# Seven quarter products in the first block's gate and up, with its background rows shared between the engines

## The reference, cut to what matters

```
hp = rms_norm(xp, norm_ffn[l]) * (1.0 + sc2_c) + sh2_c
hs = rms_norm(xs, norm_ffn[l]) * (1.0 + sc2_s) + sh2_s
xp = xp + g2_c * swiglu(hp, w_gate[l], w_up[l], w_down[l])
xs = xs + g2_s * swiglu(hs, w_gate[l], w_up[l], w_down[l])
swiglu = (silu(h @ w_gate) * (h @ w_up)) @ w_down
```

## Time and profile before

| | |
|---|---|
| median of three runs | 1569.83 us |
| profiled execution, first to last instruction | 1566.4 us |
| TensorE busy | 1538.6 us, 98% |
| VectorE busy | 1113.9 us, 71% |
| ScalarE busy | 743.6 us, 47% |
| GpSimd busy | 287.6 us, 18% |
| mean granted clock of TensorE | 0.995 |

### The profile page before, as it was taken

The page is one execution under the profiler, slowest core; times in us unless marked ns, Lnnn a source line. Parts: engine busy times, 40 slices in busy tenths (PEclk is TensorE's granted clock), DMA queues, the critical chain, the costliest instruction groups (busy, mean ns, idle before and its releaser), DMA issues.

```text
span 1566.4 us, 26496 instructions
## 1 busy us (share of the span) xinstructions
PE 1538.6 (98%) x10775; PEld 1483.5 (95%) x10775; DVE 1113.9 (71%) x1882; ACT 743.6 (47%) x1236; POOL 287.6 (18%) x344
## 2 busy tenths in 40 slices
PE   8989999999999999999999999999999999999998
PEld 6989788899999999999999899989999999999998
DVE  5657877866779746665467999988688468568453
ACT  3435555653544423442235766676365335335332
POOL 0010111000156524453253023221000000000000
PEclk9999999999999999999999999999999999999999
DMA  9332332132354544444333388875203222222322
GB/s 329 110 109 62 110 103 82 36 122 81 96 168 148 162 128 127 155 136 135 113 116 95 78 180 174 175 151 132 81 28 101 88 81 75 88 81 75 91 68 78
DMA packets 142464, 178.12 MB, mean 114 GB/s; under 512 B 13025, under 2 KB 121257, under 8 KB 141320
## 3 DMA queue, kind: packets, MB, share of 16 engines
q1 hardware_dynamic: 120128, 109.68, 22.3%
q0 software_dynamic: 21888, 66.66, 17.2%
q10 hardware_dynamic: 328, 0.10, 0.0%
HBM read 148.93 MB, written 2.79 MB: 97 GB/s over the span
## 4 chain that ended last, share of the span: by engine, by line
PE 87%; DVE 8%; ACT 2%; issue 1%; DMA 1%; POOL 0%; DVEq 0%; ACTq 0%
PE PS L777 23%; PE PS L779 22%; PE PS L782 22%; PE PS L858 5%; PE PS L860 5%; PE PS L859 5%; PE PS L1185 1%; PE PS L1196 1%; PE PS L1138 1%; DVE PTL L2698 1%; DMA MODA<-in_w_mod 1%; DVE WL L2099 0%; PE PS L1161 0%; DVE TMP L2288 0%; DVE X L2441 0%
## 5 line engine op out<-in xcount | busy, mean ns | idle before, releaser
L777 PE MATMUL PS<-HH,WH 128*128 128x320 f32 (+1 forms) x1168 | 269.6, 312 | 2.8 <-DVE HL L2299 2.2
L779 PE MATMUL PS<-HL,WH 128*128 128x320 f32 (+1 forms) x1168 | 266.1, 309 | 0.0
L782 PE MATMUL PS<-HH,WL 128*128 128x320 f32 (+1 forms) x1168 | 265.4, 308 | 0.0
L2425 DVE SCALAR_TENSOR_TENSOR X<-PS,MODV,X 128x128 f32<-128x128 f32 (+2 forms) x216 | 81.6, 434 | 185.4 <-PE PS L782 185.3
L777 PEld LDWEIGHTS PS<-HH,WH 128*128 128x128 f32 x1168 | 194.5, 188 | 7.5 <-issue 3.5
L779 PEld LDWEIGHTS PS<-HL,WH 128*128 128x128 f32 x1168 | 196.0, 188 | 0.0
L782 PEld LDWEIGHTS PS<-HH,WL 128*128 128x128 f32 x1168 | 195.8, 188 | 0.0
L2099 DVE TENSOR_TENSOR WL<-RAW,WH 128x2048 fp32r<-128x2048 f32 (+2 forms) x56 | 126.6, 2261 | 65.1 <-ACT WH L1503 64.9
L777 PE MATMUL PS<-HIDH,WH 128*128 128x320 f32 x704 | 163.0, 312 | 0.3 <-DVE HIDL L2356 0.3
L1867 ACT ACTIVATE BGW<-BGW,SC 128x512 f32<-128x512 f32 x112 | 80.8, 723 | 173.4 <-DVE BGACC L2247 124.0
L699 POOL TENSOR_TENSOR BGACC<-BGACC,BGW 128x512 f32<-128x512 f32 x97 | 132.4, 1365 | 159.8 <-ACT BGW L1867 158.6
(11 more groups left out here) (409 smaller groups left out, 3206.0 us busy)
## 6 DMA issues: line engine op xcount, KB each, us to landing
BGW<-in_w_mod POOLq DMA_DIRECT2D x112, 256.0 KB, 3.0
RAW<-in_ffn_w_gate SPq DMA_DIRECT2D x22, 1024.0 KB, 5.3
RAW<-in_ffn_w_up SPq DMA_DIRECT2D x22, 1024.0 KB, 5.4
MODA<-in_w_mod POOLq DMA_DIRECT2D x48, 256.0 KB, 3.7
RAW<-in_ffn_w_down SPq DMA_DIRECT2D x16, 768.0 KB, 4.7
RAW<-in_ffn_w_down SPq DMA_DIRECT2D x8, 1024.0 KB, 5.1
RAW<-in_conv_w_pw SPq DMA_DIRECT2D x16, 512.0 KB, 5.3
WL<-RAW POOLq DMA_DIRECT2D x8, 1024.0 KB, 9.8
```

Source lines behind the costliest of these rows:

```text
L777: mm(o, wh, xh, start=first, stop=False)
L779: mm(o, wh, xl, start=False, stop=False)
L782: ins = mm(o, wl, xh, start=False, stop=last)
L2425: ins = V.scalar_tensor_tensor(out=X[:, m, t:t + b - a], in0=tile2(n)[:, bank, a:b], scalar=g, in1=X[:, m, t:t + b - a], op0=ALU.mult, op1 ...
```

## The change

Layer 0's block gets the form of layer 1's: seven quarter products from `up 2` on, 19 units in all, the block ring, chunks of 6, 6, 6 and 4, and eight hidden places. `RING_GAP` skips three places of the ring before the last chunk, so that the ring ends where the next stage's units begin.

The 14 background halves are no longer made by VectorE, ScalarE and GpSimd together.

- 8 halves go through TensorE, 6 in layer 0 and 2 in layer 1. Inside a gate unit, after product 0 and after product 5, four column groups multiply four loaded pieces (`half_rows`). VectorE transposes the result (`turn_half`), and four small matmuls after product 3 of the up unit add it up (`turn_half_rows`). GpSimd loads the pieces to four buffers (`half_loads`); the next four are loaded when the last four have been used.
- 6 halves go as three parts of 1024 columns, one beside each of layer 0's first three chunks of down. VectorE makes the context's sum (`part_first`), ScalarE scales (`part_scaled`), and GpSimd issues a transfer that adds the scaled piece to a sum in SBUF (`part_rows`). It waits for that transfer before it loads a further piece. The three buffers `BGW` share memory with `P5`, `TMP` and `ACTV`, so ScalarE waits for adding transfers before it copies into these (`added`).
- The last half's sum before `pw2`, with two clock-holding matmuls, becomes ten clock-holding matmuls.

```diff
-DOWN_K = ((8, 8, 6), (6, 6, 6, 4))
+DOWN_K = ((6, 6, 6, 4), (6, 6, 6, 4))
-FAST_FROM = (1, 2)
+FAST_FROM = 2
+RING_GAP = 3
+PE_HALVES = {(0, 4): 0, (0, 6): 1, (0, 10): 8, (0, 12): 9, (0, 16): 10, (0, 18): 11, (1, 4): 12, (1, 6): 13}
+PART_AFTER = (8, 14, 20)
+PE_BEFORE = (2, 4, 6)
...
+            if b == last_chunk:
+                place += RING_GAP
...
# GpSimd
+            def half_loads(first, last):
+                for i in range(KT * first, KT * last):
+                    r, k = divmod(i, KT)
+                    if i >= MOD_SLOTS:
+                        pool.wait_ge(sem("modb_used"), (i - MOD_SLOTS) // GROUPS + 1)
+                    l, c0 = divmod(FIRST_BG * D + PE_ORDER[r] * 512, 6 * D)
+                    pool.dma_start(MODB[i % MOD_SLOTS][:], w_mod[l, k * P:(k + 1) * P, c0:c0 + 512]).then_inc(sem("modb_landed"), 16)
+            def part_load(q, k):
+                l, c0 = divmod((PART0 + q) * D, 6 * D)
+                pool.dma_start(BGW[k % 3][:], w_mod[l, k * P:(k + 1) * P, c0:c0 + D]).then_inc(mod_landed[k % 3], 16)
+            def part_rows(q):
+                pool.wait_ge(sem("hid_ready"), PART_AFTER[q])
+                for k in range(3):
+                    part_load(q, k)
+                for k in range(KT):
+                    pool.wait_ge(sem("bgw_scaled"), KT * q + k + 1)
+                    if k:
+                        pool.dma_start(BGACC[1][:], BGW[k % 3][:], accum_op=ALU.add).then_inc(sem("bgw_added"), 16)
+                        pool.wait_ge(sem("bgw_added"), 16 * ((KT - 1) * q + k))
+                    if k + 3 < KT:
+                        part_load(q, k + 3)
# TensorE, in fast_pair
+                def between(i):
+                    if turn is not None and i == 3:
+                        turn_half_rows(tile2(n2), turn)
+                    if part is not None and i == 3:
+                        part_sums(tile2(n2), part)
+                    if rows is not None and i in (0, 5):
+                        half_rows(tile2(n2), rows, i // 5)
+            def half_rows(ps, j, step):
+                for g in range(GROUPS):
+                    k = GROUPS * step + g
+                    i = KT * PE_ORDER.index(j) + k
+                    if g == 0:
+                        pe.wait_ge(sem("modb_landed"), 16 * (i + GROUPS))
+                    ins = mm(ps[COLG * g:COLG * (g + 1), 1, :], SC[:, k, :], MODB[i % MOD_SLOTS][:], start=(step == 0), stop=(step == 1))
+                ins.then_inc(sem("modb_used"), 1)
# ScalarE, in fast_copies
+                def added(k):
+                    if l == 0 and a in PART_AFTER:
+                        act.wait_ge(sem("bgw_added"), 16 * ((KT - 1) * PART_AFTER.index(a) + k))
                 else:
+                    added(5 if kind == "gate" else KT - 1)
                     first_copied(u)
...
+                added(KT - 2)
                 copied(u, 3, P5[q % 2][:], ps1[:, 1, 0:HALF])
+            def part_scaled(q, k):
+                act.wait_ge(sem("bgw_first"), KT * q + k + 1)
...
+                A((BGW[k % 3] if k else BGACC[1])[:], BGW[k % 3][:], ACT.Copy, scale=SC[:, k, 1:2]).then_inc(sem("bgw_scaled"), 1)
# in the down step, the same spread on ScalarE and VectorE (output tile m: pieces k)
+                                for k in ((), (0,), (1,), (2,), (3,), (4,), (5,), (6, 7))[m]:
+                                    part_scaled(a, k)
# VectorE
+            def part_first(q, k):
+                dve.wait_ge(mod_landed[k % 3], 16 * (N_ROWS * KT // ROW_SLOTS + BG_USES[k % 3] * q + k // 3 + 1))
+                acc, w, c = BGACC[0][:], BGW[k % 3][:], SC[:, k, 0:1]
...
+                    ins = V.scalar_tensor_tensor(out=acc, in0=w, scalar=c, in1=acc, op0=ALU.mult, op1=ALU.add)
+            def part_turned(q, s):
...
+                for h in range(2):
+                    link(V.transpose(BGTURN[:].rearrange("p i g c -> p (i g c)"), BGACC[s][:, 512 * h:512 * (h + 1)]))
+                    ins = V.tensor_reduce(out=BGSUM[:, s, 4 * h:4 * h + 4, :], in_=BGTURN[:], op=ALU.add, axis=mybir.AxisListType.X)
# TensorE before pw2
-            last_half_sum()
-            hold_clock(tile2(("mh", N_HALF - 1)), 2)
+            hold_clock(spare, 10)
```

More of the change, by code:

```diff
@@ L57 @@
 FIRST_SCALED = (0, 4)
-HID_SLOTS = (10, 8)
+HID_SLOTS = 8
+HID_ROOM = 10
 UNIT = 2048
@@ L390, in program @@
         REC8 = small("REC8", [P, QT])
+        BGTURN = sb("BGTURN", [P, 4, GROUPS, COLG], R_BG + 4096)
+        BGSUM = small("BGSUM", [P, 2, KT, GROUPS])
+        MODB = [sb(f"MODB{i}", [P, 512], R_ROOT + 2048 * i) for i in range(MOD_SLOTS - 1)] + [sb("MODB3", [P, 512], R_BG)]
+        BGACC = [sb("BGACC0", [P, D], R_ROOT), sb("BGACC1", [P, D], R_BG)]
+        BGW = [sb(f"BGW{i}", [P, D], R_MOD + 2 * quarter + 4096 * i) for i in range(3)]
+        assert R_MOD + 2 * quarter + 3 * 4096 <= R_T[6]
         assert top[0] <= nc.sbuf_usable_end
@@ L538, in low_there @@
             else:
[L539 to L553, removed]
+                eng.wait_ge(lo_done, plain_before(u) - sum(moved[:u]))
         def ring(w, b):
-            s = (b + RING_AT % 2 * RING // 2) % RING
-            return w[:].rearrange("p s (q n) -> p (s q) n", n=BLOCK)[:, s, :]
+            return w[:].rearrange("p s (q n) -> p (s q) n", n=BLOCK)[:, slot[b], :]
         def four(ap):
@@ L676, in _ @@
                     move_parts(j + 1)
[L677 to L700, removed]
@@ L702, in unit_low @@
+            for q, n in enumerate(PE_BEFORE):
+                if q:
+                    pool.wait_ge(sem("bg_summed"), q)
+                half_loads(PE_BEFORE[q - 1] if q else 0, n)
+                part_rows(q)
             def unit_low(i):
@@ L1882, in ffn @@
                 spread_copy(("rb", n), RSTD, QT)
-                if l == FAST_FROM[0]:
-                    whole_tiles(l)
-                else:
-                    apply(n, l, 1, lambda k: first_copy(("gate", l, 1), ACTV[1], 1) if k == 2 else None)
+                whole_tiles(l)
                 round_units(U[("up", l, 0)] + 1)
-                for step, (kind, a, f0) in enumerate(ffn_steps(l)):
-                    rows = bg_steps(l, step)
-                    if kind == "pair" and fast(U[("gate", l, a)]):
+                for kind, a, f0 in ffn_steps(l):
+                    if kind == "pair" and a > FAST_FROM:
                         fast_copies(U[("gate", l, a)])
@@ new lines, in part_read @@
+            def part_read(q, ps):
+                dve.wait_ge(sem("part_picked"), q + 1)
+                l, part = divmod(PART0 + q, 6)
+                src = ps[:, 1, 0:2 * KT].rearrange("p (s k) -> p k s", s=2)
+                b = VT1[:, V1["b_mod"] + 48 * l + 8 * part:V1["b_mod"] + 48 * l + 8 * part + 8]
+                for s in range(2):
+                    ins = V.tensor_tensor(MODV[:, l, s, 8 * part:8 * part + 8], src[:, :, s], b, ALU.add)
+                link(ins)
+                mod_gains(l, part)
@@ L2364, in fast_posts @@
                 up = kind == "up"
+                rows, turn, part = bg_half(l, kind, a), bg_turn(l, kind, a), bg_part(l, kind, a)
                 dst = TMP if up else ACTV
@@ L2743, in residuals @@
                         gain_low(norm_name, m - 1, nl, half)
-                        if step is not None and l == 0 and m < KT - 1:
-                            half_steps(1)
-                    if m % 2 == 0 and not (l == FAST_FROM[0] and step is not None):
+                    if m % 2 == 0 and chunk is None:
                         split_units(U[name(m)] + 1)
@@ L2804, in ffn @@
                             hidden_low(l, a + j, j)
-                        if a + 2 == FT:
-                            half_steps(rows[3])
                     else:
-                        residuals(lambda m: ("down", l, a, m), l, 5, "mix1" if l == 0 and a == len(DOWN_K[0]) - 1 else None, step)
+                        residuals(lambda m: ("down", l, a, m), l, 5, "mix1" if l == 0 and a == len(DOWN_K[0]) - 1 else None, a)
             ffn(0)
```

473 lines of the change are left out of this document (246 added, 227 removed).

## The result

The changed kernel takes 1603.36 us (median of four runs, 1601.26 to 1604.77), the kernel before 1568.27 on the same chips. The ratio is 1.0221, with a 95% interval of 1.0205 to 1.0238: slower by 2.2%. The forecast was 1583, slower, with a range up to 1602. The sign was right, the size was not.

The account below looks back on a forecast made before the run. TensorE, busy nearly all the time, was taken as the bound. Terms of -33.4, -4.9, -3.5, -0.5, +17.6, +4.2, -1.1, +3.6 and +31 gave +13.0 on a 1566.4 span, 1579.4; plus 3.4 for the median, 1583 us, range 1553 to 1602.

Parts of the forecast that it names:

- 19 fast units: In layer 0, 19 more units run seven products instead of eight quarter products, saving 1.76 us each: -33.4 us.
- small matmuls and old waits that go: On TensorE, 13 groups of small matmuls go (-4.9 us), and old waits with their slow clock (-3.5 and -0.5).
- 16 steps of `half_rows`: Eight halves move to TensorE, two steps each at 1.1 us: +17.6 us, bounds 14.4 to 19.2.
- 11 small sums: On TensorE, 8 `turn_half_rows` and 3 `part_sums` at 0.38 us each: +4.2 us.
- starts of the fast form: First fast gate units: layer 0 gains a 1.5 us wait, layer 1 loses 1.1 and the clock's 1.5: net -1.1 us.
- gap of three places: Layer 0's last up unit: late rounding and copy cost 1.2 us for each of three products: +3.6 us, bounds 0 and 6.
- three parts: Product 2 of gates 8, 14 and 20 waits 8.8 us, plus 1.5 at lower clock: 3 x 10.3 = +31 us.
- period of 7.1: On GpSimd's queue, a load and an add repeat every 7.1 us, against 5.28 us at which pieces are made.
- bound of 9.1: GpSimd's period if each add takes 2 us longer: a wait of 18 us, 58.5 us for the three parts.
- The adds keep pace: Rival: GpSimd's period at most 5.3 us, a wait of 1.9, +31 becomes +5.7; 1558 us, faster. Chance 0.27.
- Contended: Rival: adding transfers contend with down's 1 MB loads, period 9.1 us; 1610 us, slower. Chance 0.10.
- Late pieces at product 5: Rival: `half_rows` pieces come late at product 5, TensorE waits 2 us each time; 1599 us. Chance 0.05.

Follow-up runs that it names:

- experiment 2: Changed kernel with each adding transfer covering 128 of its 1024 columns (64 KB instead of 512 KB): 1571.29 us, single run.
- experiment 6: Changed kernel with VectorE making both sums of the parts, one piece per output tile from the first on, no scaling or adding transfers: 1571.92 us.
- 3: Changed kernel with one piece beside each output tile from the first on, instead of none beside the first and two beside the last: 1581.59 us.
- 9: Changed kernel with the 1 MB load of up units 8, 14 and 20 held back until the part's fifth add has landed: 1605.31 us.
- 4: Changed kernel with `RING_GAP` at 0 instead of 3, so no skipped ring places ahead of the last chunk: 1607.05 us.
- Experiment 5: Changed kernel, gap kept, with ScalarE and VectorE preparing four blocks ahead instead of seven in layer 0's last up unit: 1595.47 us.
- experiment 8: Changed kernel with both sums on VectorE, lead of four, and the first segment's turn moved after the next gate unit's work: 1560.68 us.
- experiment 7: Changed kernel with both sums on VectorE and a lead of four blocks in layer 0's last up unit: 1566.73 us.

## Why the prediction was wrong in size

Point by point, by its own terms, against 33.0 us more of span:

| term | forecast | measured |
|---|---|---|
| 19 fast units | -33.4 | as forecast: six units of layer 0, 541.39 to 636.03, are 94.6 us = six of layer 1's 12.28 + 15.0 of the first long wait + 4 x 1.2 + 3 x 0.38 |
| small matmuls and old waits that go | -8.9 | not measured apart |
| 16 steps of `half_rows` | +17.6 | +19.1: one is 1.19 (443.35 to 444.58, less 0.15, and 0.11 behind it) |
| 11 small sums | +4.2 | 0.38 each, as forecast |
| starts of the fast form | -1.1 | +0.9: each of the two starts has two waits, 1.46 and 0.80, with some 0.1 of restart behind each, and the old 2.63 with its 1.5 is gone; the second wait was not foreseen |
| gap of three places | +3.6 | +3.7 in up 20 (0.91, 1.10 and 1.10 with their restarts), **and +3.9 more** for HIDL in down |
| three parts | +31 | **+43.9** |

The differences are 12.9, 3.9, 2.0 and 1.5, which takes 13.0 to 33.3.

**The step that failed is the size of the wait at the chunk ends**, in the term that was sized at 3 x 10.3. The mechanism is shown: with 7/8 of the adds' bytes gone the waits are 2 us (experiment 2), with the adds gone and the pieces begun earlier none is left at product 2 (6), with an earlier start alone they shrink (3). The period of 7.1 was nearly right for what it described: undisturbed, adds follow in 7.3 to 7.6 (9). What was wrong is that the 1 MB load of up was given 0.9 us of the engines once. It is issued with the second add, and the next issue behind that add comes after 8.6 to 11.0 us. Held back, it leaves waits of 9.3 to 9.7, where the forecast had 8.8. The rest of the 13.3, 11.1 and 14.0 is this meeting: 4.0, 1.4 and 4.5 us. So of the 12.9 us that the term lacked, some 9.9 are the meeting, 2.1 the undisturbed chain (its first interval is 6.6 to 6.8 where 5.2 was taken) and 1.0 a slow clock that lasted longer. What the meeting costs hangs on the moment: in experiments 4 and 5, whose programs are the same up to the third chunk end, the load goes out between 0.2 before and 0.8 behind the second add, whose next issue comes after 7.2 to 10.8 us, and the waits are 9.4 to 13.7. The bound of 9.1 for the period was thought of as all adds contended; in truth one was, and strongly.

That the chain ends in piece 7's load and not in the fifth add made little difference, since both come at the same moment. As a reason it was still misplaced: by these rows, who had taken the add's wait out of ScalarE's program alone would have gained next to nothing. No run tries it.

**Slips in the working.** The sum counts the 0.6 us between the fifth add's landing and a next issue, for which the copy does not wait: the landing is at D0 + 52.6 and not 53.2. The bounds are not what four periods of 6.4 and 9.1 give: that is a wait of 6.0 instead of 5.0, and 16.8 instead of 18. The low end by the terms that it names is 1551 and not 1553. And in the earlier trace rows it is VectorE that has a third of layer 0 to spare; ScalarE and GpSimd have 60%. None of these decides anything.

**The gap's term was half of it.** It looked only at TensorE's waits inside the unit. VectorE stands in the same order: it handles the late blocks ahead of the last multiplications, and so HIDL's operation began 3.2 us later against down's start than at the first chunk (4.6 in place of 1.4), and TensorE waited 3.6. Experiment 5 removes both by asking for less lead, and changes nothing else: the cost wasn't the gap but a lead larger than the ring then has room for.

**The rivals.** "The adds keep pace", to which 0.27 was given, is refuted: the first five adds of a part are issued 6.3 to 11.6 us apart. Its price was too low as well: it called a wait of 1.9 too short to lower the clock much, but in experiment 2 the waits of 2.15, 1.81 and 1.81 have a slow clock behind them, 1.3, 1.5 and 1.5 us of it. The rule of the Trainium skill (DMA: Bandwidth & Descriptors, section "Anatomy of one DMA — SWDGE (gpsimd) path"), about 2.0 us plus the bytes at 436 GB/s, gives 3.2 us for 512 KB and 2.15 for 64 KB. These traces disagree: the least of 21 landings of 512 KB was 4.5 and the median 6.2, and the median for 64 KB was 3.2. "Contended" was nearest to the truth in time (1610) with a chance of 0.10. "Late pieces at product 5" is refuted: TensorE has no wait for `MODB` in layer 0's block of the changed kernel.

**Where the gain of the fast form went.** Its 33 us are there. 23 went to `half_rows` and its small sums, work that idle engines had done before. 44 went to three waits. With the three waits and the gap's out, and `half_rows` still paid, the same form of the block is 8 us faster than the kernel before (experiment 8).

## What to carry to other kernels

Before a step is put in a chain of "wait for the landing, issue the next", compare the chain's whole period with the pace of the work beside it, and then lay the other queues' issue times over it: one 1 MB load at the wrong moment cost 1.4, 4.0 and 4.5 us here. A loop through an engine's own operation (1.27 us) beats one through a transfer (7.3 us) even where the engine is 70% busy, if its order leaves the urgent work in front. A lead that is right on average is wrong where the buffer is short: set it per unit.

## What was not expected of the hardware

- Adding transfers of 512 KB from SBUF to SBUF, each behind a load of its size, follow each other in 7.3 to 7.6 us undisturbed. Beside a 1 MB load one takes 8.6 to 11.0 to the next issue, where it takes 6.7 without it.
- VectorE's operation with two tensors of 1024 columns takes 1.27 us, and up to 3.2 beside a GpSimd addition, which itself goes from 2.4 to 3.8.
- After a wait of 2.3 us the clock's answer differed. The first windows below are of experiments 6 and 7, behind the same wait in the same place; up to there the two programs are the same and differ by 1.4 us in phase. The granted clock was 0.50 in one and 1.00 in the other, while behind experiment 7's other two waits of that size it was at the lower level too. The wait of 3.58 for HIDL has 1.00 behind it in the changed kernel (864 to 867) and 0.50 in experiment 6 (832.5 to 835), and one of 1.81 has 0.52 behind it in experiment 2. Waits of 2 to 4 us can't be priced with one number; why is open.

```profile
552.00:555.00 3.00, 2.83 (x10) 2.83 (x11) 3.00 (x6) 1.91 (x5) 0.00 (x0) 0.50 0.55 192
...
553.00:556.00 3.00, 2.42 (x16) 2.42 (x17) 3.00 (x7) 1.91 (x6) 0.00 (x0) 1.00 0.71 248
...
674.00:677.00 3.00, 3.00 (x14) 3.00 (x13) 2.96 (x5) 2.30 (x5) 0.86 (x1) 0.52 0.24 30
```
